# Turning y, output projection, first norm and first feed-forward products in one stage

## The chip, the core and the metric

One Trainium2 chip, one of its cores. The engines are TensorE (PE, matmuls; PEld is its weight load), VectorE (DVE), ScalarE (ACT), GpSimd (POOL) and the sync engine's queue (SP), all working from queues of their own and meeting at semaphores. The metric is the time on the device of one execution of the whole program, in microseconds; lower is better.

## What is computed

Two layers of a hybrid backbone over 9 tiles of 128 tokens (8 of a sample, 1 of a prompt), model width 1024, feed-forward width 4096, all in float32. The part that matters here is the end of a layer:

```
y   = concat(attn 512 | mlstm 256 | gmlp 256) @ w_out
x   = LayerNorm(alpha * x + gate1 * y)
h2  = x * (1 + scale2) + shift2
x   = LayerNorm(alpha * x + gate2 * (relu(h2 @ w_ff1)^2 @ w_ff2))
```

Before it stand the modulation of x, one combined input projection z = h @ w_in, a two-way mLSTM scan, a gated spatial MLP and an attention with axial rotary.

## The kernel before

A product in float32 is made of three matmuls of rounded parts (`product`, L1489): hi*hi, hi*lo and lo*hi. So each operand exists as `hi` (a copy rounded by ScalarE) and `lo` (the difference, by VectorE or GpSimd). Weights come through a ring of four raw slots on SP's queue (L448); `split_hi` (L402, ScalarE) and `split_lo` (L412, VectorE) make the two parts of the eight slots of 128x512 of a group. A slot is refilled once the last tile has used it.

`dense` (L1497) multiplies one tile of 128 tokens by one group: 8 x 3 matmuls of 512 columns into one PSUM bank.

Each layer is cut into eight stages by `phase` (L354): every engine drains, counts up a semaphore, and waits until all four have. The stages that the change touches:

- Stage 1 is the input projection and the mLSTM. GpSimd's queue ends it with the load of zq (L549).
- Stage 2 is the gating part. VectorE takes means and variances of `vn`; GpSimd raises `rs` to the power -0.5 (L478), drains, and makes `nbias` (L554); ScalarE normalises with these, then VectorE and TensorE go on (L1166, L1633).
- Stage 5: TensorE turns y, tile by tile with eight transposes (L1774), ScalarE copies to `hi` (L842), VectorE subtracts to `lo` (L1343). All of y is turned before the barrier.
- Stage 6: GpSimd issues the loads of x (`xr`), of the gates and of `lnb` (L601 to L608). TensorE runs `dense` over the nine tiles for the left half of the output columns, then for the right half. VectorE's `residual` (L1349) makes gate * y and alpha * x + that. After the right half comes the norm, spread over three engines: statistics on VectorE (L949), power and `nbias` on GpSimd (L480), x * rs + nbias on ScalarE (L664), gain on GpSimd (L491), offset on VectorE (L960), store of x1 on GpSimd (L610). Then TensorE turns x (L1788), VectorE modulates it out of PSUM with eight operations a tile (L935), ScalarE rounds (L660), GpSimd subtracts (`lo_of`, L495). There are three bank pairs for turned tiles.
- Stage 7 is the feed-forward in eight chunks of 512 hidden columns. GpSimd begins it with a memset of `acc` (L622), for which VectorE waits before its first hidden tile. `first_product` (L1800) makes twelve blocks of 128 hidden columns by 384 tokens; `second_product` (L1819) makes 18 blocks that VectorE adds to `acc` (`summed`, L1390). After the last chunk comes the second norm with the same helpers as the first, tile by tile, with three banks for TensorE to run ahead; tiles are stored by `store2` (L640).

The order of work on each engine is written out by hand and is the order of the program text. A queue is strictly in order.

Of the kernel before, what the change touches and what calls it, by code (L numbers as in the profile page):

```python
# [17 lines left out]
ALU = mybir.AluOpType  # L18
# [5 lines left out]
P = 128  # L24
# [146 lines left out]
def build(nc, x_in, cond, w_mod, m_slots, b_mod, w_slots, consts, rope, cache_k, cache_v, state0, row_in,  # L171
# [6 lines left out]
    with ExitStack() as ctx:  # L178
# [33 lines left out]
        xr = put("xr", [NT, D])  # L212
        hf2 = put("hf2", [3, D])
        lnb = put("lnb", [2, D])
        gate = put("gate", [2, D])
        lnt = put("lnt", [2, W])
        put = region(a_b + NT * D * 4, a_a)
        f_hi = put("f_hi", [HC // P, TOK], F32R)
        f_lo = put("f_lo", [HC // P, TOK], F32R)
        fr = put("fr", [2, GRP])  # L220
        fsq = put("fsq", [2, GRP])

# [103 lines left out]
        def sem(name):  # L326
# [12 lines left out]
            yT_ps y_hi y_lo o_out xr_half ln_ld xr_done x1_st  # L339
            h_ps r_done fhi_done flo_done f_ps f_acc acc_zero ln_in ln_rs ln_x ln_g y_rdy ln_st""".split()  # L340
# [6 lines left out]
        NB = 8  # L347
# [104 lines left out]
        def _(pool):  # L452
# [27 lines left out]
            def norm_rows(L, w, x, gain, store):  # L480

                for t in range(NT + 2):
                    if t < NT:
                        n, r = NT * (2 * L + w) + t, rs[:, t:t + 1]
                        pool.wait_ge(S["ln_in"], n + 1)
                        pool.tensor_tensor(r, r, half[:, 0:1], ALU.pow)
                        pool.drain()  # L487
                        pool.tensor_tensor(nbias[:, t:t + 1], nmean[:, t:t + 1], r, ALU.mult).then_inc(S["ln_rs"], 1)
                    if 1 <= t <= NT:
                        pool.wait_ge(S["ln_x"], NT * (2 * L + w) + t)  # L490
                        pool.tensor_tensor(x[:, t - 1], x[:, t - 1], gain, ALU.mult).then_inc(S["ln_g"], 1)  # L491
                    if t > 1:
                        store(t - 2)
# [7 lines left out]
            for L in range(NL):  # L501
# [49 lines left out]

                rstd(L, 0, rs[:].unsqueeze(2), 1)
# [46 lines left out]
                phase(pool, L, 5)  # L599

                pool.dma_start(xr[:], (y_out if L else x_in).rearrange("t p d -> p t d")).then_inc(S["ln_ld"], 16)  # L601
                pool.wait_ge(S["mod_st"], stored(L))
                for g in range(2):
                    for n in range(2):
                        pool.dma_start(gate[:, g, n * W:(n + 1) * W],
                                       gate_dram[L, 0, g, n * W:(n + 1) * W].partition_broadcast(P)).then_inc(S["ln_ld"], 16)
                for k in range(2):
                    pool.dma_start(lnb[:, k], ln_gb[L, k].partition_broadcast(P)).then_inc(S["ln_ld"], 16)  # L608

                def store1(t):  # L610
                    pool.wait_ge(S["xr_done"], NT * L + t + 1)
                    own(pool)
                    pool.dma_start(x1_dram[t], xr[:, t]).then_inc(S["x1_st"], 16)

                norm_rows(L, 0, xr, lnb[:, 0], store1)

                for t in range(NT):
                    lo_of(t, hf2[:, t % 3], 2 * NT * L + NT + t)
                pool.wait_ge(S["x1_st"], 16 * NT * (L + 1))
                phase(pool, L, 6)  # L620
# [24 lines left out]
                pool.wait_ge(S["ln_ld"], 16 * (13 * L + 13))  # L645
                norm_rows(L, 1, acc, lnb2[:, 0], store2)
                pool.wait_ge(S["ln_st"], 16 * NT * (L + 1))
                phase(pool, L, 7)
# [3 lines left out]
        def _(act):  # L652
# [11 lines left out]
            def norm_rows(L, w, x):  # L664

                for t in range(NT):
                    act.wait_ge(S["ln_rs"], NT * (2 * L + w) + t + 1)
                    act.activation(x[:, t], x[:, t], ACT.Identity, bias=nbias[:, t:t + 1],
                                   scale=rs[:, t:t + 1]).then_inc(S["ln_x"], 1)
# [37 lines left out]
            for L in range(NL):  # L707
# [131 lines left out]
                for t in range(NT):  # L839
                    act.wait_ge(S["yT_ps"], NT * L + t + 1)  # L840
                    for k in range(2):
                        ins = act.copy(hi[:, 4 * k:4 * k + 4, t * P:(t + 1) * P],  # L842
                                       ps[:, 2 * (t % 3) + k, :].rearrange("p (a b) -> p a b", b=P))
                    ins.then_inc(S["y_hi"], 1)
                phase(act, L, 5)

                split_hi(act, L, 6, (S["o_out"], START + 18 * L + 9))
                norm_rows(L, 0, xr)
                for half_, tiles in ((0, range(3)), (1, range(3, NT))):
                    split_hi(act, L, 7, (S["o_out"], START + 18 * L + 18), range(RAW * half_, RAW * half_ + RAW))  # L850

                    for t in tiles:
                        hi_of(t, hf2[:, t % 3], 2 * NT * L + NT + t)
                phase(act, L, 6)


                def hidden(i, b):
# [5 lines left out]
                    act.activation(f_hi[:, b // 3, (b % 3) * GRP:(b % 3 + 1) * GRP], fr[:, b % 2],  # L863
# [15 lines left out]
                norm_rows(L, 1, acc)  # L879
                if L < NL - 1:  # L880
                    split_hi(act, L, 2 * NFF + 7, (S["f_ps"], START + 18 * NFF * (L + 1)))
                phase(act, L, 7)
# [3 lines left out]
        def _(dve):  # L886
# [62 lines left out]
            def statistics(x, t):  # L949

                dve.drain()
                for j in range(2):
                    dve.bn_stats(st6[:, t, j], x[:, t, j * W:(j + 1) * W])
                dve.drain()
                dve.bn_aggr(mv[:, t], st6[:, t].rearrange("p a b -> p (a b)"))
                dve.drain()
# [8 lines left out]
            for L in range(NL):  # L965
# [394 lines left out]
                for t in range(NT - 1):  # L1360
                    residual(0, t)
# [572 lines left out]
```

## Time and profile before

| | us |
|---|---|
| median of 3 runs | 3694.7 (3691.9 to 3694.89) |
| the profiled execution | 3692.73 |
| its span in the trace | 3690.8 |
| TensorE busy / VectorE / ScalarE / GpSimd | 3205.9 / 1743.1 / 914.2 / 593.4 |

Times in the rows are microseconds from the span's start unless "ns" stands there. Layer 0's stages 5 and 6 lie between 822 and 1000 us, its last chunk with the second norm ends at about 1900; layer 1's lie between 2671 and 2848, and its end is the end of the program. TensorE runs at one of two clocks, 1.2 or 2.4 GHz, and the granted clock averages 0.923 of the full one over the span. A matmul's end is modelled, so the pace of a run is read from the distance of two starts.

### The profile page before, as it was taken

To read this page: it belongs to the slowest core of one execution; us is meant where nothing else is said; L and a number is where in the kernel's file an instruction comes from. 1 tells how busy PE (TensorE), PEld (TensorE's weight loads), DVE (VectorE), ACT (ScalarE), POOL (GpSimd) and SP (SyncE) were. 2 spreads that over 40 slices of the span, in tenths; PEclk is the share of its full clock that TensorE was granted. 3 is DMA by queue.
4 is the path that set the end of the run, shared out by engine and by line. 5 is a ranking of instruction groups with operands and counts; after the bars stand their busy time and mean duration, and the time that the engine had idled before them with its cause. 6 is when DMAs were issued, how large, how long until landed. Compare 5 with 4: busy or idle time off the path is not lost.

```text
span 3690.8 us, 44939 instructions
## 1 busy us (share of the span) xinstructions
PE 3205.9 (87%) x17192; PEld 2577.7 (70%) x17192; DVE 1743.1 (47%) x3144; ACT 914.2 (25%) x1688; POOL 593.4 (16%) x635
## 2 busy tenths in 40 slices
PE   5999649989599999999849996499995999999995
PEld 4778534447488888889838785344474999999994
DVE  4444366654733333333583443666447333333337
ACT  2222124441212211112222221244412222222221
POOL 2010133321600000000150001333216000000004
PEclk7999759999799999999979997599897999999998
DMA  5431300002122222221311113000021111111112
GB/s 191 153 112 52 99 10 1 0 0 103 70 78 81 79 76 76 85 84 35 114 68 34 52 52 99 10 1 0 0 97 74 44 37 35 46 46 46 46 46 114
DMA packets 100547, 225.71 MB, mean 61 GB/s; under 512 B 13168, under 2 KB 13744, under 8 KB 99856
## 3 DMA queue, kind: packets, MB, share of 16 engines
q1 hardware_dynamic: 78240, 151.76, 13.2%
q0 software_dynamic: 22128, 71.50, 5.2%
q8 instruction: 121, 1.98, 0.2%
q14 instruction: 58, 0.48, 0.0%
HBM read 194.33 MB, written 28.87 MB: 60 GB/s over the span
## 4 chain that ended last, share of the span: by engine, by line
PE 67%; issue 11%; DVE 9%; POOL 6%; DMA 3%; POOLq 2%; ACT 2%; DVEq 1%; ACTq 0%; SPq 0%
PE ps L1491 18%; PE ps L1495 17%; PE ps L1494 17%; PE ps L1686 3%; DVE hf L940 2%; PE ps L1665 2%; PE ps L1473 2%; DVE nm L1294 1%; POOL acc L491 1%; PE ps L1676 1%; POOL xr L491 1%; POOLq L487 1%; PE ps L1579 1%; PE ps L1677 1%; PE ps L1633 1%
## 5 line engine op out<-in xcount | busy, mean ns | idle before, releaser
L1491 PE MATMUL ps<-hi,w_hi 128*128 128x384 f32 x1584 | 539.2, 340 | 62.8 <-POOLq L357 44.4
L1495 PE MATMUL ps<-hi,w_lo 128*128 128x384 f32 x1584 | 533.1, 337 | 0.0
L1494 PE MATMUL ps<-lo,w_hi 128*128 128x384 f32 x1584 | 532.7, 336 | 0.0
L1491 PE MATMUL ps<-w_hi,f_hi 128*128 128x512 f32 x1152 | 459.4, 399 | 34.7 <-DVE acc L1395 34.7
L1494 PE MATMUL ps<-w_lo,f_hi 128*128 128x512 f32 x1152 | 453.0, 393 | 0.0
L1495 PE MATMUL ps<-w_hi,f_lo 128*128 128x512 f32 x1152 | 452.4, 393 | 0.0
L410 ACT CAST w_hi<-w_raw 128x512 fp32r<-128x512 f32 x368 | 214.4, 619 | 909.8 <-PE ps L1491 805.7
L1491 PE MATMUL ps<-w_hi,hi 128*128 128x512 f32 (+1 forms) x1008 | 393.0, 390 | 15.1 <-DVE xr L1356 7.4
L1395 DVE TENSOR_TENSOR acc<-acc,ps 128x512 f32<-128x512 f32 x288 | 196.0, 685 | 419.2 <-PE ps L1495 419.0
L1494 PE MATMUL ps<-w_lo,hi 128*128 128x512 f32 (+1 forms) x1008 | 384.3, 381 | 0.0
L1495 PE MATMUL ps<-w_hi,lo 128*128 128x512 f32 (+1 forms) x1008 | 383.9, 381 | 0.0
L415 DVE TENSOR_TENSOR w_lo<-w_raw,w_hi 128x512 fp32r<-128x512 f32 x368 | 261.8, 751 | 200.7 <-ACT w_hi L410 200.3
L1491 PEld LDWEIGHTS ps<-hi,w_hi 128*128 128x128 f32 x1584 | 300.4, 190 | 75.1 <-issue 55.9
L1384 DVE TENSOR_TENSOR fsq<-fr 128x384 f32<-128x384 f32 x192 | 107.0, 557 | 482.7 <-ACT fr L861 482.5
L1494 PEld LDWEIGHTS ps<-lo,w_hi 128*128 128x128 f32 x1584 | 300.2, 189 | 0.5
L1495 PEld LDWEIGHTS ps<-hi,w_lo 128*128 128x128 f32 x1584 | 299.9, 189 | 0.0
L1491 PEld LDWEIGHTS ps<-w_hi,f_hi 128*128 128x128 f32 x1152 | 218.7, 190 | 94.5 <-DVE acc L1395 39.8
L1495 PEld LDWEIGHTS ps<-w_hi,f_lo 128*128 128x128 f32 x1152 | 218.5, 190 | 46.6
L1494 PEld LDWEIGHTS ps<-w_lo,f_hi 128*128 128x128 f32 x1152 | 218.6, 190 | 43.4
L802 ACT ACTIVATE pr<-ps 128x512 f32<-128x512 f32 x292 | 171.2, 598 | 272.9 <-PE ps L1677 270.0
L1491 PEld LDWEIGHTS ps<-w_hi,hi 128*128 128x128 f32 x1008 | 194.1, 193 | 58.6 <-DVE xr L1356 8.3
L861 ACT ACTIVATE fr<-ps 128x384 f32<-128x384 f32 x192 | 94.2, 491 | 517.6 <-PE ps L1495 517.6
(268 smaller groups left out, 4389.8 us busy)
## 6 DMA issues: line engine op xcount, KB each, us to landing
w_raw<-in_w_slots SPq DMA_DIRECT2D x368, 256.0 KB, 3.2
w_raw<-in_m_slots SPq DMA_DIRECT2D x160, 256.0 KB, 2.8
x_dram<-xr POOLq DMA_DIRECT2D x18, 512.0 KB, 3.0
x1t<-x_dram POOLq DMA_DIRECT2D x6, 1536.0 KB, 14.9
out<-acc POOLq DMA_DIRECT2D x18, 512.0 KB, 3.0
modw<-in_w_mod SPq DMA_DIRECT2D x4, 2048.0 KB, 9.8
acc<-in_x_in SPq DMA_DIRECT2D x3, 1536.0 KB, 16.8
zq_dram<-stg POOLq DMA_DIRECT2D x18, 256.0 KB, 2.3
```

What stands on the lines that cost most here:

```text
L410: act.copy(w_hi[:, j, :], w_raw[:, j % RAW, :]).then_inc(S["w_hi_done"], 1)
L415: dve.tensor_tensor(w_lo[:, j, :], w_raw[:, j % RAW, :], w_hi[:, j, :].bitcast(F32), ALU.subtract).then_inc(S["w_lo_done"], 1)
L491: pool.tensor_tensor(x[:, t - 1], x[:, t - 1], gain, ALU.mult).then_inc(S["ln_g"], 1)
L802: act.activation(pr[:, j if nk > 1 else g], ps[:, 3 + (j + g) % 2, :], ACT.Exp).then_inc(S["ex_done"], 1)
L861: act.activation(fr[:, b % 2], ps[:, b % 3, 0:GRP], ACT.Relu).then_inc(S["r_done"], 1)
L940: ins = dve.tensor_scalar(dst[:, u, kt * P:(kt + 1) * P], ps[:, 2 * u + kt // 4, (kt % 4) * P:(kt % 4 + 1) * P], col(L, which, 1, kt, g), ...
L1384: dve.tensor_tensor(fsq[:, b % 2], fr[:, b % 2], fr[:, b % 2], ALU.mult)
L1395: dve.tensor_tensor(a, a, ps[:, 3 + s_ % 3, :], ALU.add).then_inc(S["f_acc"], 1)
L1491: mm = pe.matmul(out, a_hi, b_hi, start=first, stop=False)
L1494: pe.matmul(out, a_hi, b_lo, start=False, stop=False)
L1495: return pe.matmul(out, a_lo, b_hi, start=False, stop=last)
L1686: return pe.matmul(ps[j:j + w, bank, :], weights, moving, start=start, stop=stop)
```

## The change

Stages 5 and 6 and the beginning of stage 7 become one stage without barriers; NB, the barriers per layer, goes from 8 to 6.

- x lives in the rows of z: its left half lies over the columns of mLSTM's q and k, which are unused after stage 1, its right half over the columns that y occupies. The left half and the gates are loaded on GpSimd's queue right after barrier 1 (`xa_ld`), the right half and `lnb` once all of y is turned (`xb_ld`).
- TensorE turns two tiles of y ahead, then one tile before each product; in the second pass it turns a tile of x after each product from the fourth on. Turned tiles have two bank pairs, (3, 4) and (5, 7). The last three tiles of x are turned inside the first feed-forward product, whose order is new (`first_blocks`): the lower halves of the sums of blocks 0 and 1, their upper halves, then block 2.
- The norm: `residual` gives the sum with `accum_out`; VectorE makes the negated mean; ScalarE squares x minus the mean with a sum (`squares`); GpSimd makes 1 / sqrt(variance + eps) (`deviation`); VectorE finishes with two fused operations (`normal`). GpSimd no longer multiplies by the gain. The second norm is changed in the same way.
- The modulation: VectorE takes the left four blocks of a tile (`modulate2`), ScalarE the right four (`modulated`).
- f_hi and f_lo lie in other places, as four tiles each.

```diff
+def first_blocks():
+    lower, upper = range(KT // 2), range(KT // 2, KT)
+    out = [(0, 0, lower), (0, 1, lower), (0, 0, upper), (0, 1, upper), (0, 2, range(KT))]
+    return out + hidden_blocks()[6:]
...
+        NB = 6
+        X_BANKS = ((3, 4), (5, 7))
...
+            def deviation(n, t):
+                r = rs[:, t:t + 1]
+                pool.wait_ge(S["ln_sq"], n + 1)
+                pool.tensor_scalar(r, r, 1.0 / D, EPS, ALU.mult, ALU.add)
+                pool.drain()
+                pool.tensor_tensor(r, r, half[:, 0:1], ALU.pow).then_inc(S["ln_rstd"], 1)
...
                 phase(pool, L, 1)
+                pool.dma_start(x_halves(0), (y_out if L else x_in).rearrange("t p d -> p t d")[:, :, 0:W]).then_inc(S["xa_ld"], 16)
+                pool.wait_ge(S["mod_st"], stored(L))
+                for g in range(2):
+                    for n in range(2):
+                        pool.dma_start(gate[:, g, n * W:(n + 1) * W],
+                                       gate_dram[L, 0, g, n * W:(n + 1) * W].partition_broadcast(P)).then_inc(S["xa_ld"], 16)
                 rstd(L, 0, rs[:].unsqueeze(2), 1)
                 pool.drain()
                 pool.tensor_tensor(nbias[:], nmean[:], rs[:], ALU.mult).then_inc(S["pow_out"], 1)
...
+                pool.wait_ge(S["yT_ps"], NT * (L + 1))
+                own(pool)
+                pool.dma_start(x_halves(1), xin[:, :, W:D]).then_inc(S["xb_ld"], 16)
...
+                for t in range(NT + 4):
+                    if t < NT:
+                        deviation(2 * NT * L + t, t)
+                    if 1 <= t <= NT:
+                        store1(t - 1)
+                    if t >= 4:
+                        lo_of(t - 4, hf2[:, t % 2], 2 * NT * L + NT + t - 4)
...
+            def squares(n, t, x, out):
+                act.wait_ge(S["ln_mu"], n + 1)
+                act.drain()
+                act.activation(out, x, ACT.Square, bias=nmean[:, t:t + 1], accum_out=rs[:, t:t + 1]).then_inc(S["ln_sq"], 1)
...
+                for t in range(NT):
+                    squares(2 * NT * L + t, t, x_row(t), sqr[:].rearrange("p (a b) -> p a b", b=W))
+                    if t == NT - 1:
+                        split_hi(act, L, 7, (S["o_out"], START + 18 * L + 18), range(RAW))
+                    if t >= 4:
+                        modulated(L, t - 4)
+                modulated(L, 5)
+                split_hi(act, L, 7, (S["o_out"], START + 18 * L + 18), range(RAW, SLOTS))
+                for t in range(6, NT):
+                    modulated(L, t)
...
+            def normal(n, t, x, weights, done):
+                dve.wait_ge(S["ln_sq"], n + 1)
+                dve.scalar_tensor_tensor(x, x, nmean[:, t:t + 1], w_row(weights, 0), ALU.add, ALU.mult)
+                dve.drain()
+                dve.wait_ge(S["ln_rstd"], n + 1)
+                dve.scalar_tensor_tensor(x, x, rs[:, t:t + 1], w_row(weights, 1), ALU.mult, ALU.add).then_inc(done, 1)
...
+                for t in range(NT):
+                    residual(1, t)
+                    negated_mean(t, mv[:, t, 0:1], mv[:, t, 1:2])
+                    if t == NT - 1:
+                        split_lo(dve, L, 7, range(RAW))
+                    if t:
+                        normal1(t - 1)
+                    if t >= 4:
+                        modulate2(L, t - 4)
+                modulate2(L, 5)
+                normal1(NT - 1)
+                split_lo(dve, L, 7, range(RAW, SLOTS))
+                for t in range(6, NT):
+                    modulate2(L, t)
...
+                y_turned(0)
+                y_turned(1)
                 for t in range(NT):
+                    if t + 2 < NT:
+                        y_turned(t + 2)
+                    pe.wait_ge(S["y_lo"], START + NT * L + t + 1)
+                    pe.wait_ge(S["xr_half"], START + 18 * L + t - 2)
+                    dense(L, 5, t, t % 3, W, t == 0, t == NT - 1, S["o_out"])
+                for t in range(NT):
+                    pe.wait_ge(S["xr_half"], START + 18 * L + 9 + t - 2)
+                    dense(L, 6, t, t % 3, W, t == 0, t == NT - 1, S["o_out"])
+                    if t >= 3:
+                        x_turned(t - 3)
...
+                        if not i and not m and not ks[0]:
+                            x_turned(6 + g)
+                            pe.wait_ge(S["h_done"], START + 2 * NT * L + NT + 3 * g + 3)
```

## Rows read from the trace of the kernel before

**Rows 1.** The page: the chain that ended last, shares by engine.
```profile
PE 67%; issue 11%; DVE 9%; POOL 6%; DMA 3%; POOLq 2%; ACT 2%; DVEq 1%; ACTq 0%; SPq 0%
```

**Rows 2.** Timeline, TensorE: start, duration, operation, [idle before and releaser].
```profile
822.36 0.63 PE L1774 MATMUL ps<-ident,zq 128*128 128x128 f32 x4 [0.91 <-DVEq L357]
823.26 0.60 PE L1774 MATMUL ps<-ident,zq 128*128 128x128 f32 x4
...
825.91 0.66 PE L1774 MATMUL ps<-ident,zq 128*128 128x128 f32 x4 [0.74 <-DVE lo L1343]
...
835.96 0.79 PE L1491 MATMUL ps<-w_hi,hi 128*128 128x512 f32 x1 [2.98 <-DVEq L357]
...
836.97 0.63 PE L1495 MATMUL ps<-w_hi,lo 128*128 128x512 f32 x1
837.40 0.63 PE L1491 MATMUL ps<-w_hi,hi 128*128 128x512 f32 x1
...
842.89 0.39 PE L1491 MATMUL ps<-w_hi,hi 128*128 128x512 f32 x1
843.11 0.39 PE L1494 MATMUL ps<-w_lo,hi 128*128 128x512 f32 x1
...
859.81 0.80 PE L1491 MATMUL ps<-w_hi,hi 128*128 128x512 f32 x1 [4.52 <-DVE xr L1356]
...
944.09 0.39 PE L1495 MATMUL ps<-w_hi,lo 128*128 128x512 f32 x1
...
999.81 0.66 PE L1491 MATMUL ps<-hi,w_hi 128*128 128x384 f32 x1 [16.63 <-POOLq L357]
```

**Rows 3.** Timeline, VectorE, layer 0's projection and norm.
```profile
858.29 0.69 DVE L1353 TENSOR_TENSOR lnt<-ps,gate 128x512 f32<-128x512 f32 x1 [22.88 <-DMA lnb<-in_ln_gb]
859.07 0.69 DVE L1356 SCALAR_TENSOR_TENSOR xr<-xr,lnt 128x512 f32<-128x512 f32 x1
...
918.09 2.38 DVE L1356 SCALAR_TENSOR_TENSOR xr<-xr,lnt 128x512 f32<-128x512 f32 x1
...
950.94 2.63 DVE L940 TENSOR_SCALAR hf<-ps,modc 128x128 f32<-128x128 f32 x8
```

**Rows 4.** Timeline, GpSimd, layer 0's norm and the feed-forward's start.
```profile
917.51 2.41 POOL L491 TENSOR_TENSOR xr<-xr,lnb 128x1024 f32<-128x1024 f32 x1
...
964.12 6.95 POOL L498 TENSOR_TENSOR lo<-hf,hi 128x1024 fp32r<-128x1024 f32 x3
...
999.72 7.79 POOL L622 MEMSET acc<- 128x9216 f32 x1 [0.52 <-POOLq L357]
```

**Rows 5.** Timeline, VectorE and GpSimd, the end of layer 0.
```profile
1820.10 1.22 DVE L1438 TENSOR_TENSOR acc<-acc,gate 128x1024 f32<-128x1024 f32 x1 [10.28 <-DMA lnb<-in_ln_gb]
...
1866.19 2.95 DVE L1438 TENSOR_TENSOR acc<-acc,gate 128x1024 f32<-128x1024 f32 x1
...
1874.80 2.98 DVE L1438 TENSOR_TENSOR acc<-acc,gate 128x1024 f32<-128x1024 f32 x1
...
1897.33 1.22 DVE L963 TENSOR_TENSOR acc<-acc,lnb 128x1024 f32<-128x1024 f32 x1 [2.23 <-POOL acc L491]
...
1804.19 2.17 POOL L632 DMA_DIRECT2D gate<-gate_dram  x4 [164.14 <-PE ps L1495]
...
1829.34 0.19 POOL L488 TENSOR_TENSOR nbias<-nmean,rs 128x1 f32<-128x1 f32 x1 [4.06 <-issue]
```

**Rows 6.** Timeline, GpSimd, the end of stage 1, layer 0.
```profile
444.64 1.08 POOL L549 DMA_DIRECT2D zq<-zq_dram  x1 [11.84 <-DMA out<-mrow]
```

**Rows 7.** The chain of waits around barrier 1, layer 0: start, duration, what.
```profile
445.72 12.62 POOLq L357
...
464.71 0.21 POOL nbias L554
```

**Rows 8.** Timeline, ScalarE, layer 0.
```profile
953.00 1.24 ACT L668 ACTIVATE xr<-xr,nbias,rs 128x1024 f32<-128x1024 f32 x1 [4.34 <-POOL nbias L488]
...
1015.81 0.49 ACT L861 ACTIVATE fr<-ps 128x384 f32<-128x384 f32 x1 [1.53 <-PE ps L1495]
```

More of the change, by code:

```diff
@@ L612, in store1 @@
                     own(pool)
[L613 to L618, printed above, removed]
+                    pool.dma_start(x1_dram[t].rearrange("p (a b) -> p a b", b=W), x_row(t)).then_inc(S["x1_st"], 16)
+                for t in range(NT + 4):
[5 more added lines that the diff above has]
+                        lo_of(t - 4, hf2[:, t % 2], 2 * NT * L + NT + t - 4)
                 pool.wait_ge(S["x1_st"], 16 * NT * (L + 1))
-                phase(pool, L, 6)
+                pool.wait_ge(S["xT_ps"], 2 * NT * (L + 1))
+                own(pool)
                 pool.memset(acc[:], 0.0).then_inc(S["acc_zero"], 1)
@@ L643, in store2 @@
                     pool.dma_start(y_out[t], acc[:, t]).then_inc(S["ln_st"], 16)
-                pool.wait_ge(S["ln_ld"], 16 * (13 * L + 13))
-                norm_rows(L, 1, acc, lnb2[:, 0], store2)
+                pool.wait_ge(S["ln_ld"], 16 * 6 * (L + 1))
+                for t in range(NT + 1):
+                    if t < NT:
+                        deviation(2 * NT * L + NT + t, t)
+                    if t > 0:
+                        store2(t - 1)
                 pool.wait_ge(S["ln_st"], 16 * NT * (L + 1))
-                phase(pool, L, 7)
+                phase(pool, L, 5)
         @block.scalar
@@ L1358, in _ @@
-                dve.wait_ge(S["ln_ld"], 16 * (13 * L + 7))
-                own(dve)
-                for t in range(NT - 1):
-                    residual(0, t)
-                split_lo(dve, L, 6)
-                residual(0, NT - 1)
-                for t in range(NT + 2):
-                    if t < NT:
-                        residual(1, t)
-                        statistics(xr, t)
-                    if t > 1:
-                        offset(L, 0, xr, t - 2, lnb[:, 1], S["xr_done"])
-                    if t >= NT - 1:
-                        modulate(L, t + 1, 1, hf2, t - (NT - 1), 1)
@@ L1428, in _ @@
                 chunk(NFF - 1)
-                for t in range(NT + 2):
+                for t in range(NT + 1):
                     if t < NT:
@@ L1440, in _ @@
                         dve.wait_ge(x1_ld[t // 3], 16 * (L + 1))
-                        dve.scalar_tensor_tensor(a, x1t[:, t], ALPHA, a, ALU.mult, ALU.add)
-                        statistics(acc, t)
-                    if t > 1:
-                        offset(L, 1, acc, t - 2, lnb2[:, 1], S["y_rdy"])
+                        dve.scalar_tensor_tensor(a, x1t[:, t], ALPHA, a, ALU.mult, ALU.add, accum_out=mv[:, t, 0:1])
+                        negated_mean(t, mv[:, t, 0:1], 0.0)
+                    if t > 0:
+                        normal(2 * NT * L + NT + t - 1, t - 1, y_row(acc, t - 1), lnb2, S["y_rdy"])
                 if L < NL - 1:
                     split_lo(dve, L, 2 * NFF + 7)
-                phase(dve, L, 7)
+                phase(dve, L, 5)
         @block.tensor
```

173 lines of the change are left out of this document (85 added, 88 removed).

## The prediction, made before the changed kernel was run

> **What bounds the kernel now.** I read the page first, its shares by engine in the chain [rows 1]: TensorE is 67% of the chain that ended last, and 11% is "issue". So only time in which TensorE stands still is for sale, and the question is where it stands. The timeline of TensorE answers it for layer 0 [rows 2]: it turns y from 822.36 us, waits 2.98 us for a barrier, multiplies from 835.96, waits 4.52 us at 859.81, ends the second half of the output projection at 944.09, and starts the feed-forward at 999.81. The first three hidden blocks are out, at about 1015.2, just before ScalarE reads the third at 1015.81 [rows 8]. The feed-forward's wait for the barrier alone is 16.63 us. Layer 1 runs through the same code and shows the same order. What stands between is VectorE, ScalarE and GpSimd work [rows 3, 4]. The end of each layer is paced by VectorE [rows 5], and the gating part's short stage by a chain through GpSimd [rows 6, 7].
>
> Two behaviours of the rows decide the sum. First, in [rows 3] a 512-wide two-input VectorE operation takes 0.69 us at 859.07 but 2.38 us at 918.09, where GpSimd's L491 [rows 4] runs from 917.51 for 2.41 us; it ends when that one ends plus its own time. So the two exclude each other. (The Trainium skill, SBUF — State Buffer, section on two separate sides, calls this an exclusive lock between a GpSimd operation and a VectorE one with two SBUF inputs; the trace agrees.) VectorE's modulation, read from PSUM, is not slowed: 0.32 us each [rows 3]. Second, GpSimd's barrier right after its zq load [rows 6] lasts 12.62 us [rows 7], until that load is in; and in [rows 5] the `nbias` at 1829.34 stands behind a drain and that is when the 6.8 MB issued from 1804.19 on (gates, x1t, lnb2: 4 x 256, 3 x 1536, 2 x 512 KB) are through. A drain on GpSimd therefore waits for the DMAs that GpSimd has issued.
>
> **The change, from 822.36 to the end of the first three hidden blocks, per layer.**
> Start. Two tiles of y are turned, 0.9 us each (822.36 to 823.26 is one tile, [rows 2]). The third needs the banks of the first, free at 825.91 as now [rows 2]. The first product starts at 826.9 instead of 835.96: -9.1. Six more turns lie among the products: 6 x 0.9 = +5.4. ScalarE's copies and VectorE's subtractions for them take 1.2 us in a tile period of over 6 and are hidden.
> x. Half of x and the gates are loaded after barrier 1, the other half with lnb once y is turned, some 30 us before the second pass. The wait for the DMA (VectorE at 858.29, [rows 3]) goes: 4.52 us. Behind it TensorE ran at 1.2 GHz (matmuls 0.43 us apart at 836.97, 0.23 at 842.89, [rows 2]) for some 13 matmuls, 13 x 0.2 = 2.6. The low clock of the very first product stays. -7.1.
> Second pass. Six tiles of x are turned in it, five before its end: +4.5. Can VectorE keep up? A tile costs it 0.77 + 0.77 for the residual, 0.2 for the mean, 2.5 for two fused 1024-wide steps (1.23 each [rows 5]; nothing shows one with a sum output, for which I take no extra, and 0.1 each at most), 1.3 for four modulations: 5.6 us against TensorE's 24 x 0.2275 + 0.9 = 6.4 (the matmuls from 842.89 on follow at 0.22 to 0.23). Turn t must wait until tile t-2 has left its two banks. ScalarE's cast closes this 6.7 us after the product's end, about one period, so it is just in time until GpSimd's `lo` of 2.32 us (three in 6.95, [rows 4]) comes in: from then VectorE's two-input steps wait for it, the cast comes after 8.5 to 8.9 us, and two or three periods grow to 7.4: +2.9. The second pass ends at 944.3 - 9.1 + 5.4 - 7.1 + 7.4 = 940.9.
> After it (T). Now: 1015.2 - 944.4 = 70.8 us. After, in VectorE's order, with four splits, 0.62 us apart, waiting for ScalarE's: residual and mean to T+1.8; squares on ScalarE to 3.2 (1.24 for 1024 wide [rows 8]); splits 0 to 3 to 6.8; norm of tile 7 to 9.4; modulation of 4 and 5 to 12.0; cast of 4 to 11.8, `lo` of 4 to 14.2, which holds back the norm of tile 8 to 16.7; GpSimd stores tile 8 before `lo` of 5, which ends at 19.7; splits 4 to 7 to 21.6; modulation of 6 and 7 to 24.2. TensorE meanwhile makes the lower half of the first block, that of the second from 19.7, their upper halves from 21.6 to 27.7 with the low clock, turns tile 8, and this is modulated to 29.9, cast to 31.0, `lo` to 33.4. The third block ends at T+37.5, at the low clock in part T+39. -31.8. ScalarE's four 128-wide steps are not in the trace: from 384 wide 0.49 and 1024 wide 1.24 [rows 8] comes an estimate of 0.2 each, at most 0.49. 0.2 is nearest and VectorE's four take longer; at 0.49 each tile of the tail costs 0.7 more.
> GpSimd's memset of acc (7.79 us [rows 4]) now overlaps TensorE: to T+41.2. VectorE waits for it before its first hidden tile, but three banks let TensorE run on to its sixth block at T+45. No cost here; if the tail came out 5 us shorter, it would begin to show.
> Sum: -9.1 + 5.4 - 7.1 + 7.4 - 31.8 = -35.2 us per layer. Bounds -42 (no exclusion in the tail) and -25 (each of five `lo` operations delays the chain once more).
>
> **The end of a layer.** Now a tile takes VectorE 8.61 us (1866.19 to 1874.80, [rows 5]), with a 2.98 us product [rows 5] held back by GpSimd's gain. That gain, the statistics (about 2.0 in five short operations) and the offset go. After: 1.37 for two sums, 1.30, 1.31, 0.2 for the mean, 2.5 for the norm: 6.7, and 0.3 for GpSimd's single-column steps on `rs` that can come between: 7.0. TensorE needs 5.46 and follows. The start stays (1820.10, [rows 5]: the load's landing). The first norm waits for the drain that ends at 1829.3, so iteration 1 ends at 1831.2; seven more at 7.0 give 1880.2, the last norm 1882.9, in place of the L963 that ends at 1898.5: -15.6. Bounds -12 and -18. ScalarE's squares lie in VectorE's next iteration. Both layers end in the same way.
>
> **Stage 2, gating norm.** The first half of x (2.36 MB) and four gates (1.05 MB) are issued on GpSimd's queue after barrier 1, and behind them stand `rs`, a drain and `nbias`, for which ScalarE, then VectorE, then TensorE wait: `nbias` at 464.71 [rows 7] is in the chain. The issues end by about 461.7 (1.08 for the large one [rows 6], 2.17 for four gates as in [rows 5]) and hide behind VectorE's statistics. The drain does not: 2.36 MB held the barrier for 13.7 us from issue, 6.8 MB held the drain 25.1 us, so 3.4 MB hold it 14 to 16 us from 458.4. `nbias` comes at about 473.2 instead of 464.7: +8.5, bounds 0 and +10. (The Trainium skill, PSUM — Partial Sum Buffer, section on engine and sequencer instructions, says that a drain waits for the engine to go fully idle, and names no DMAs. By it this term would be 0 and the forecast 17 us lower; [rows 5, 7] speak against that reading.)
> Two barriers go; their waits are counted above.
>
> **The sum.** -35.2 - 15.6 + 8.5 = -42.3 per layer, -85 for both. Profiled execution: 3692.7 us (span 3690.8) gives 3607.7; the median of the runs, 3694.7, stands 2 us higher, so 3610.
>
> **The rivals.**
> A: the drain does not wait for DMAs (a large DMA only holds a barrier). Then stage 2 costs nothing: 3610 - 17 = 3593. For it: only one long drain outside a barrier is among the rows. Against: its end falls on the end of the transfers. Chance 0.12.
> B: the exclusion and the two bank pairs bite harder. Each x turn waits for cast and `lo` in series, the second pass goes at 9 us a tile for five tiles, and the tail gets five delays: -25 and -12 in place of -35.2 and -15.6, 13.8 a layer, 3638. For it: both orders are strict and every engine waits for another. Against: the PSUM reads and ScalarE do not contend. Chance 0.2.
> C, slower: the clock. The merged stage's stops are short but frequent. If the clock stayed at 1.2 GHz throughout, 432 matmuls would cost 0.2 us more each, 86 us a layer. It decides from half of them: 43 us a layer cancel the gain. All of them would give 3610 + 2 x 86 = 3782; the likely form of this case, six tenths of them, 3713. Against: the stop of 2.98 us in [rows 2] lowered it for under 7 us (835.96 to 842.89), and the stops expected here are shorter. Chance 0.03.
> D: the tail does not shorten, since the feed-forward's start hangs on tile 8 anyway: it takes 55 us in place of 39. Then -19.2 in the merged stage: 3642. Against: only the third block needs tile 8, and 8 us of products come before. Chance 0.1.
> The forecast has 0.55.
>
> **How the numbers follow.** Range: A at 3593 less the better bounds gives 3575 at the outside, B and D with stage 2 at its upper bound 3645. With 2 in 10 left out: 3580 to 3640. All cases but C are faster by far more than 0.2%, about what a measurement of this kernel can tell from none. Faster 0.96, same 0.01, slower 0.03.
>
> **What would show it.** Between the second pass's last product and the third hidden block some 39 us; no TensorE wait for a DMA in the merged stage; second-pass periods of 6.4 growing to 7.4; `nbias` of stage 2 some 8 us later, behind GpSimd's drain; VectorE's last tiles 7.0 us apart, and no GpSimd operation 1024 wide among them. The prediction is wrong if TensorE waits over 1.5 us at each turn of x, if the low clock covers over a third of the merged stage, or if VectorE's fused steps with a sum take clearly more than 0.69 and 1.23 us.

## The result: 3595 us, inside the range

| | before | after |
|---|---|---|
| median (runs) | 3693.3 (4) | 3595.1 (4; 3590.7 to 3599.8) |
| span of the profiled execution | 3690.8 | 3588.9 |
| TensorE / VectorE / ScalarE / GpSimd busy | 3205.9 / 1743.1 / 914.2 / 593.4 | 3168.6 / 1680.1 / 939.4 / 529.0 |

The ratio is 0.9739, with a 95% interval of 0.9719 to 0.9759. The forecast was 3610, the range 3580 to 3640. All times in this text are of fast executions; one execution below, the profiled one of the kernel with two waits less, was a slow one (10900.3 us beside 3553.0 to 3556.4 for its other five), so its trace is not read. On the page the chain that ended last, by engine, reads now (before: [rows 1]):

```profile
PE 73%; DVE 8%; issue 7%; POOL 3%; DMA 3%; ACT 2%; POOLq 2%; DVEq 1%; ACTq 0%; SPq 0%
```

TensorE has more of the chain and "issue" less, as a kernel with fewer stops should show. TensorE is also busy for 37 us less with the same products and turns: from the first turn of y to the third hidden block of layer 0 its granted clock averages 0.94, where it was 0.82.

**The merged stage, layer 0.** TensorE's timeline (start, duration, operation, [idle before and releaser]) answers [rows 2]:

```profile
833.26 0.63 PE L1847 MATMUL ps<-ident,zq 128*128 128x128 f32 x4 [0.91 <-DVEq L400]
...
837.66 0.47 PE L1563 MATMUL ps<-w_hi,hi 128*128 128x512 f32 x1
...
838.44 0.40 PE L1563 MATMUL ps<-w_hi,hi 128*128 128x512 f32 x1
...
839.13 0.40 PE L1563 MATMUL ps<-w_hi,hi 128*128 128x512 f32 x1
...
943.33 1.06 PE L1855 MATMUL ps<-ident,xr 128*128 128x128 f32 x8 [1.20 <-ACT hi L708]
...
950.82 1.06 PE L1855 MATMUL ps<-ident,xr 128*128 128x128 f32 x8 [0.96 <-ACT hi L708]
961.11 1.94 PE L1855 MATMUL ps<-ident,xr 128*128 128x128 f32 x8 [9.23 <-ACT hi L708]
...
969.38 0.44 PE L1563 MATMUL ps<-hi,w_hi 128*128 128x384 f32 x1 [2.22 <-POOL lo L534]
...
982.38 0.69 PE L1563 MATMUL ps<-hi,w_hi 128*128 128x384 f32 x1 [5.13 <-POOL lo L534]
...
988.68 0.44 PE L1563 MATMUL ps<-hi,w_hi 128*128 128x384 f32 x1
```

Read it as three stretches. From the first turn of y (833.26) to the first product (837.66) there are 4.4 us. To the last product's end at 949.9 (the T of the prediction) it is 116.6 us from the start. From there to the end of the third hidden block at 988.4, just before the fourth begins at 988.68, it is 38.5 us. TensorE waits for no DMA on the way. In all 155.1 us, where the kernel before took 193.4 (822.36 to 1015.8, where ScalarE begins to read the third block, [rows 2, 8]): -38.3. The prediction put that end at 1015.2, 0.6 us too early.

What sets the pace in the second pass is in VectorE's and GpSimd's timelines; the first of each group answers to [rows 3] and [rows 4]:

```profile
920.51 0.69 DVE L1416 TENSOR_TENSOR lnt<-ps,gate 128x512 f32<-128x512 f32 x1 [2.03 <-PE ps L1567]
...
926.84 0.69 DVE L1416 TENSOR_TENSOR lnt<-ps,gate 128x512 f32<-128x512 f32 x1 [0.71 <-PE ps L1567]
927.61 2.61 DVE L1419 SCALAR_TENSOR_TENSOR xr<-xr,lnt 128x512 f32<-128x512 f32 x1
930.15 0.08 DVE L1419 DVE_READ_ACCUMULATOR xr<-xr,lnt 128x1 f32 x1
...
934.29 0.68 DVE L1416 TENSOR_TENSOR lnt<-ps,gate 128x512 f32<-128x512 f32 x1
...
942.16 0.69 DVE L1416 TENSOR_TENSOR lnt<-ps,gate 128x512 f32<-128x512 f32 x1
...
943.86 3.10 DVE L1015 SCALAR_TENSOR_TENSOR xr<-xr,nmean,lnb 128x1024 f32<-128x1024 f32 x1
```

```profile
927.30 2.38 POOL L534 TENSOR_TENSOR lo<-hf,hi 128x1024 fp32r<-128x1024 f32 x1 [0.93 <-ACT hi L708]
...
943.28 2.60 POOL L534 TENSOR_TENSOR lo<-hf,hi 128x1024 fp32r<-128x1024 f32 x1 [1.15 <-ACT hi L708]
...
979.98 2.35 POOL L534 TENSOR_TENSOR lo<-hf,hi 128x1024 fp32r<-128x1024 f32 x1 [2.17 <-ACT hi L708]
982.26 7.79 POOL L664 MEMSET acc<- 128x9216 f32 x1
```

The residuals of successive tiles begin 6.33, 7.45 and 7.87 us apart. The 2.61 us operation at 927.61 stands in for one of 0.69, and it ends at 930.22, 0.54 us after GpSimd's `lo` of 927.30 is through (929.68). The same stands at 943.86: 3.10 for 1.28, under the `lo` of 943.28.

**The end of layer 0**, VectorE [rows 5]:

```profile
1793.03 1.23 DVE L1510 TENSOR_TENSOR acc<-acc,gate 128x1024 f32<-128x1024 f32 x1 [10.69 <-DMA lnb<-in_ln_gb]
...
1802.93 1.29 DVE L1018 SCALAR_TENSOR_TENSOR acc<-acc,rs,lnb 128x1024 f32<-128x1024 f32 x1 [1.89 <-POOL rs L529]
...
1818.73 1.22 DVE L1510 TENSOR_TENSOR acc<-acc,gate 128x1024 f32<-128x1024 f32 x1
...
1825.34 1.23 DVE L1510 TENSOR_TENSOR acc<-acc,gate 128x1024 f32<-128x1024 f32 x1
...
1852.16 1.28 DVE L1018 SCALAR_TENSOR_TENSOR acc<-acc,rs,lnb 128x1024 f32<-128x1024 f32 x1 [0.46 <-POOL rs L529]
```

A tile takes 6.61 us in place of 8.61, none of its two-input operations is stretched (the longest takes 1.29 us for one), and the stretch from the first tile to the last norm is 60.4 us instead of 78.4: -18.0.

**Stage 2, layer 0**, the chain of waits in order of time (start, duration, what), which answers [rows 7]:

```profile
446.93 1.07 POOL zq L585
448.00 13.72 POOLq L400
...
462.41 1.02 POOL xr L588
463.43 2.18 POOL gate L592 x4
...
466.05 1.89 POOLq L595
467.94 6.71 issue
...
474.68 0.20 POOL nbias L596
```

The power ends at 467.94, and for 6.71 us nothing of the chain runs: GpSimd stands in its drain while the x and gate loads are under way. Layer 1 shows the same, 6.81 us. Below, this time between the power and `nbias` is called the hold.

The balance is -38.3 - 18.0 + 6.6 = -49.7 us for layer 0. For layer 1 the same three places give about -37.2, -19.4 and +6.7. That is -99.6 us of the span's -101.9. The good fit is in part chance: outside the three places layer 0 came out 4.6 us longer and layer 1 6.9 us shorter. Most of that lies ahead of stage 2 or in stages 3 and 4, and single profiles scatter there: kernels that share all code up to the load of zq issue it in layer 0 anywhere from 444.75 to 451.80. What moved these stretches is not settled.

### The profile page after: what moved, and what is told of

It is laid out like the page before. It is cut to its first block, busy times and chain, and to the rows that moved or that the text cites. A ratio compares the mean times of both kernels' runs of the same rounds, so it can differ in the third digit from the quotient of the medians.

```text
span 3588.9 us, 44827 instructions
## 1 busy us (share of the span) xinstructions
PE 3168.6 (88%) x17192; PEld 2549.8 (71%) x17192; DVE 1680.1 (47%) x3018; ACT 939.4 (26%) x1796; POOL 529.0 (15%) x601
## 4 chain that ended last, share of the span: by engine, by line
PE 73%; DVE 8%; issue 7%; POOL 3%; DMA 3%; ACT 2%; POOLq 2%; DVEq 1%; ACTq 0%; SPq 0%
PE ps L1563 20%; PE ps L1567 19%; PE ps L1566 19%; PE ps L1758 3%; PE ps L1737 2%; PE ps L1545 2%; DVE nm L1359 1%; PE ps L1748 1%; DVE hf L998 1%; PE ps L1651 1%; PE ps L1749 1%; PE ps L1705 1%; POOL dg L620 1%; PE ps L1674 1%; PE ps L1669 1%
## 5 line engine op out<-in xcount | busy, mean ns | idle before, releaser
L458 DVE TENSOR_TENSOR w_lo<-w_raw,w_hi 128x512 fp32r<-128x512 f32 x368 | 246.7, 711 | 201.9 <-ACT w_hi L453 201.5
```

What stands on the lines that cost most here:

```text
L458: dve.tensor_tensor(w_lo[:, j, :], w_raw[:, j % RAW, :], w_hi[:, j, :].bitcast(F32), ALU.subtract).then_inc(S["w_lo_done"], 1)
```

## Experiments

What each should tell apart. My theory has four parts: the drain pays for loads that are under way (term +8.5); the exclusion between GpSimd's `lo` (the subtraction that makes the low half of a tile) and VectorE is what stretches the second pass; the fused norm pays at the end of the layer; the new order of the first blocks is what shortens the tail. The ratios are all against the kernel before, run beside each kernel on the same chip; the kernel before itself had medians of 3684.9 to 3692.5 us there, so medians from different chips differ by some us for that alone.

**The kernel after once more**, as the reference for the small differences.

> The changed kernel as it is, on the same chip as the next three, for differences of less than 1%. Every theory: about 3595 us as before, and in stage 2 of both layers a hold of 6.7 us at GpSimd's drain between the power of rs and nbias.

Measured: 3593.9 us, ratio 0.9739 (0.9720 to 0.9759), holds of 7.33 us in layer 0 and 6.89 in layer 1. The numbers of the result stand.

**The loads behind `nbias`.**

```diff
-pool.dma_start(x_halves(0), ...).then_inc(S["xa_ld"], 16)
-...
 rstd(L, 0, rs[:].unsqueeze(2), 1)
 pool.drain()
 pool.tensor_tensor(nbias[:], nmean[:], rs[:], ALU.mult)
+pool.dma_start(x_halves(0), ...).then_inc(S["xa_ld"], 16)
+...
```

> The five loads of x's left half and the gates are issued after nbias instead of before rs. Theory (GpSimd's drain waits for the DMAs that GpSimd has issued): the hold of 6.7 us per layer goes, the loads now end behind the 22 us of stage 2, so 13 us less than the changed kernel. Rival (the drain is long for another reason, or the time comes back at barrier 2 or with the loads of stage 3): within 3 us of the changed kernel.

Measured: 3580.9, ratio 0.9698 (0.9677 to 0.9719), so 13.1 us less than the kernel after. The drain now takes 0.16 us. This shows that the loads ahead of the drain cost the time, but not how: they could slow the engine's work, or the drain could wait for them.

**The loads stay, the drain goes.** The power counts a semaphore and `nbias` waits for this.

```diff
-rstd(L, 0, rs[:].unsqueeze(2), 1)
-pool.drain()
+rstd(L, 0, rs[:].unsqueeze(2), 1).then_inc(S["own_p"], 1)
+pool.wait_ge(S["own_p"], L + 1)
```

> The loads stay before rs; between the power and nbias GpSimd waits for a semaphore that the power itself counts up, instead of a drain. Theory (the drain waits for the DMAs, not for the engine's own operation): nbias follows the power within 0.3 us although the loads are in flight; 13 us less than the changed kernel, as with late loads. Rival (traffic of 3.4 MB slows GpSimd or the visibility of its results, whichever way it waits): nbias stays some 6 us behind the power, no gain.

Measured: 3577.8, ratio 0.9697 (0.9678 to 0.9716), 16.2 us less than the kernel after. GpSimd's timeline, with the loads in flight:

```profile
462.16 1.02 POOL L588 DMA_DIRECT2D xr<-in_x_in  x1 [13.91 <-POOLq L400]
463.18 2.17 POOL L592 DMA_DIRECT2D gate<-gate_dram  x4
465.85 1.84 POOL L521 TENSOR_TENSOR rs<-rs,half 128x9 f32<-128x9 f32 x1 [0.50 <-DVE rs L1225]
467.78 0.20 POOL L596 TENSOR_TENSOR nbias<-nmean,rs 128x9 f32<-128x9 f32 x1
```

`nbias` follows the power at once although 3.4 MB are moving. The two holds of the kernel after sum to 14.2 us, near enough to the 16.2 (15.5 by the ratios). So the traffic slows nothing in this chain; it is the drain that waits. Rival A of the prediction (the drain doesn't wait for DMAs) is refuted, and the Trainium skill's words on the drain (PSUM — Partial Sum Buffer, section on engine and sequencer instructions), read as naming the engine's work alone, don't cover this case.

**Only the gates behind `nbias`**, a dose: 2.36 MB are in front of the drain in place of 3.4.

> Only the four gate loads (1.05 of 3.41 MB) move behind nbias, x's left half stays before rs. Theory (the hold lasts until the issued bytes are in, at some 0.4 MB a us): 1.05 MB is 2.6 us of transfer, so the hold falls from 6.7 to 3.5 to 4.5 us and the kernel gains 4 to 6 us over both layers. Rival (a fixed cost of any drain behind a DMA): the hold stays 6.7 us. Rival (it is the partition-broadcast of the gates that is slow): the hold falls to under 1 us.

Measured: 3584.7, ratio 0.9723 (0.9702 to 0.9744); holds of 4.46 and 4.01 us. GpSimd in layer 0:

```profile
459.08 1.02 POOL L588 DMA_DIRECT2D xr<-in_x_in  x1 [13.26 <-POOLq L400]
462.77 1.84 POOL L521 TENSOR_TENSOR rs<-rs,half 128x9 f32<-128x9 f32 x1 [2.67 <-DVE rs L1225]
469.07 0.21 POOL L591 TENSOR_TENSOR nbias<-nmean,rs 128x9 f32<-128x9 f32 x1 [4.46 <-issue]
```

The trace has the one load in front of the drain land 9.8 us after its issue at 459.08, at 468.9, and `nbias` starts 0.2 us later; in layer 1 it is 9.4 us from 2250.53, and `nbias` starts at 2260.06, 0.1 us later. So the hold ends with the landing. 1.05 MB fewer take 2.9 us off each hold, about what the transfer of these needs at the 0.4 MB a us of this stretch. The time fell by 9.3 us and the holds by 5.75; the rest is within what two kernels' medians leave open (about 4 us).

**The second norm alone**, put into the kernel before.

```diff
 for t in range(NT + 1):
     ...
-    dve.scalar_tensor_tensor(a, x1t[:, t], ALPHA, a, ALU.mult, ALU.add)
-    statistics(acc, t)
+    dve.scalar_tensor_tensor(..., accum_out=mv[:, t, 0:1])
+    negated_mean(t, mv[:, t, 0:1], 0.0)
+    if t > 0: normal(NT * L + t - 1, t - 1, ...)
```

> The kernel before with one part of the change: the second norm in fused form (sum in the residual, squares on ScalarE, two fused steps on VectorE, no gain on GpSimd). Theory: the end of each layer is VectorE's and its tiles go from 8.6 to 6.6 us; 18 us per layer as in the changed kernel's trace, so some 36 us less than the kernel before (0.990). Rival (the gain at a layer's end needs the merged stage, through x1's earlier stores or loads): under 20 us less.

Measured: 3644.7 beside 3684.9, ratio 0.9883 (0.9865 to 0.9901): -40 us by the medians, -43 by the ratio and -36 at the interval's weak end. The end of layer 0 on VectorE:

```profile
1823.46 1.23 DVE L1478 TENSOR_TENSOR acc<-acc,gate 128x1024 f32<-128x1024 f32 x1 [10.03 <-DMA lnb<-in_ln_gb]
...
1882.55 1.28 DVE L998 SCALAR_TENSOR_TENSOR acc<-acc,rs,lnb 128x1024 f32<-128x1024 f32 x1 [0.46 <-POOL rs L509]
```

From the first tile's start to the last norm's end at 1883.83 it is the 60.4 us of the kernel after again. This norm alone is over a third of the whole gain, and it is independent of the merged stage.

**`lo` of the turned x tiles on VectorE**, not on GpSimd, so that no 1024-wide GpSimd operation stands in the stage.

```diff
-lo_of(t - 4, hf2[:, t % 2], 2 * NT * L + NT + t - 4)      # GpSimd
+dve.tensor_tensor(lo[:, :, t * P:(t + 1) * P], hf2[:, t % 2], hi[...], ALU.subtract)
```

> The changed kernel with the subtraction hi to lo of the nine x tiles in the merged stage on VectorE (1.2 us each) instead of GpSimd (2.3 us and held or holding). Theory (GpSimd and VectorE exclude each other, so GpSimd's operation costs VectorE its whole length anyway): second pass about as now, the piece from its last product to the third hidden block shrinks from 38.6 to about 34 us, 6 to 12 us less than the changed kernel in all. VectorE's two-input steps of 2.6 to 3.2 us are gone. Rival (VectorE is simply full, and GpSimd's work was mostly beside it): 5 us or more slower than the changed kernel.

Measured: 3584.4, ratio 0.9722 (0.9704 to 0.9739) beside 0.9739. By the medians some 10 us are gone and by the ratios 6, but the intervals overlap, so the trace must decide. In it no two-input operation of VectorE in this stage takes over 1.29 us, the subtraction takes 1.22 us where GpSimd's took 2.4 to 3.5, and the last wait of TensorE is shorter (3.96 us in place of 5.13):

```profile
962.32 1.94 PE L1867 MATMUL ps<-ident,xr 128*128 128x128 f32 x8 [10.38 <-ACT hi L706]
...
980.17 0.45 PE L1575 MATMUL ps<-hi,w_hi 128*128 128x384 f32 x1 [3.96 <-DVE lo L1438]
```

The third block ends 36 us after the last product in place of 38.5, and the second pass ends 1.4 us earlier; its periods are 6.36, 7.06, 7.49 and 7.08. From the first turn of y to the fourth block it is 151.7 us in place of 155.4, in layer 1 149.9 in place of 154.5. So the exclusion is real, but getting rid of it in this way brings only some 4 us a layer, since the moved work costs VectorE 1.22 us a tile. The periods still grow to 7.1 and more, so the exclusion is not all that stretches the second pass: VectorE's own work fills these tiles. No run takes the exclusion away without giving VectorE more to do, so what it costs by itself is not measured.

**The old order of the hidden blocks**, in the merged stage.

```diff
-hidden_blocks() if i else first_blocks()
+hidden_blocks()
```

> The changed kernel with the first feed-forward product in the old order of blocks (three lower halves, then three upper halves). Theory (only block 2 needs tile 8, and whatever is queued behind its wait comes late): the upper halves of blocks 0 and 1, 2 x 2.1 us, move behind the wait for the last lo, 4.2 us per layer, 8 us slower than the changed kernel. Rival (the start of the feed-forward hangs on tile 8 alone): no change beyond 2 us.

Measured: 3597.3, ratio 0.9760 (0.9743 to 0.9776), +3.4 us by the medians and +7.8 by the ratios. TensorE's wait for tile 8 is 6.40 us, and the upper halves of blocks 0 and 1 stand behind it:

```profile
980.57 0.69 PE L1563 MATMUL ps<-hi,w_hi 128*128 128x384 f32 x1 [6.40 <-POOL lo L534]
```

ScalarE reads the third block at 992.41, 42.4 us after the last product. The order is worth 2 to 4 us a layer of a tail that was 71 us in the kernel before; most of the shortening comes without it.

**All eight modulation steps on VectorE.**

```diff
-for kt in range(KT // 2): dve.tensor_scalar(hf2[...], ps[...], ...)
-for kt in range(KT // 2, KT): act.activation(hf2[...], ..., ACT.Identity, bias, scale)
+for kt in range(KT): dve.tensor_scalar(hf2[...], ps[...], ...)
```

> The changed kernel with all eight modulation steps of a tile on VectorE, none on ScalarE. Theory (VectorE's queue is the longest chain in the second half of the pass and in the piece after it): 1.3 us more in some three periods of the pass and in five tiles after it, 8 to 12 us per layer, 16 to 24 us slower than the changed kernel. Rival (the waits are set by ScalarE's cast and its four slower steps of 1.49 us, so sharing gives little): under 6 us slower.

Measured: 3612.1, ratio 0.9796 (0.9779 to 0.9813), +18.2 by the medians and +21 by the ratios. TensorE's waits at the turns grow, and two more turns run at the low clock (1.90 and 1.94 us for 1.06):

```profile
927.49 1.06 PE L1849 MATMUL ps<-ident,xr 128*128 128x128 f32 x8 [1.83 <-ACT hi L708]
...
936.10 1.90 PE L1849 MATMUL ps<-ident,xr 128*128 128x128 f32 x8 [2.08 <-ACT hi L708]
...
954.21 1.94 PE L1849 MATMUL ps<-ident,xr 128*128 128x128 f32 x8 [2.98 <-ACT hi L708]
965.37 1.94 PE L1849 MATMUL ps<-ident,xr 128*128 128x128 f32 x8 [9.22 <-ACT hi L708]
```

Here VectorE is the bound of the second pass, with 8.6 to 9.5 us a tile. The share given to ScalarE is a large part of what makes the merged stage fit: undoing it costs the merged stage some 9 us a layer, twice what taking `lo` to VectorE gained.

**A better version.** If drains on GpSimd wait for its transfers, the barrier behind stage 1 loses most: there the drain stands behind the 2.36 MB load of zq, for 12.62 us in the kernel before [rows 6, 7] and 13.72 in the one after. Four kernels follow it up, each on top of the last, and the first on top of the kernel with its own semaphore. First the load of zq goes behind `nbias`.

```diff
-pool.dma_start(zq[:], ...).then_inc(S["zq_ld"], 16)
 phase(pool, L, 1)
 rstd(...); pool.wait_ge(S["own_p"], L + 1); pool.tensor_tensor(nbias[:], ...)
+pool.dma_start(zq[:], ...).then_inc(S["zq_ld"], 16)
```

> The kernel after with GpSimd's power counted by a semaphore of its own (as in e2_own_semaphore) and, in addition, the load of zq (2304 KB) issued behind the negated bias and no longer just ahead of the barrier that ends stage 1. In the traces so far GpSimd issues this load at 446.93 and its drain in the barrier ends 13.7 us later (12.6 in layer 1), when the load lands; VectorE idles 18.4 us in front of stage 2. Theory (a drain on GpSimd waits for the DMAs that GpSimd issued): with no load in flight the drain takes about 0.6 us, VectorE starts stage 2 about 14 us earlier in each layer, the load hides behind stage 2 (22 us long, while 5.8 MB take about 15 us at the 390 GB/s of this stretch), so -26 to -28 us against e2_own_semaphore: about 3550. Rival (the barrier itself takes 12 us after a long stage, or another engine comes last): the drain stays above 10 us and the time stays near 3578. Second rival (5.8 MB do not land in time): the load hides badly, the barrier behind stage 2 is held up to 10 us, 3560 to 3572.

Measured: 3561.0, ratio 0.9646 (0.9633 to 0.9659), 16.7 us less than the kernel with its own semaphore by the medians and 19 by the ratios, against the 26 to 28 of the theory. The chain of waits tells where the rest is:

```profile
436.78 12.48 DMA out<-mrow
...
449.48 5.63 POOLq L400
...
455.24 0.43 DVE st L1219
```

GpSimd's last store has landed (449.26) and the zq load is not yet issued, still its drain takes 5.63 us, and 3.66 in layer 1. From the issue of that store to stage 2's first operation it is 18.5 and 17.2 us now, against 27.6 and 28.0 with the load in front: 9.1 and 10.8 us gained. The direction is confirmed; the size was wrong, because I took the whole of the drain for the load's. The second rival (the load hides badly) is refuted: the next barrier comes 28.2 us after stage 2's start, as before.

Then two waits at the end of the layer: the drain between the two steps of each `deviation`, and VectorE's wait for the second norm's weights, which now stands at the first operation that reads them.

```diff
-pool.tensor_scalar(r, r, 1.0 / D, EPS, ALU.mult, ALU.add)
-pool.drain()
+pool.tensor_scalar(...).then_inc(S["own_d"], 1)
+pool.wait_ge(S["own_d"], n + 1)
...
-dve.wait_ge(S["ln_ld"], 16 * 6 * (L + 1))
+dve.wait_ge(S["ln_ld"], 16 * 4 * (L + 1))
...
+if t == 1: dve.wait_ge(S["lnb_ld"], 16 * 2 * (L + 1))
```

> e9_zq_late with two more waits of the end of the layer taken away: GpSimd's drain between the two steps of each deviation is a semaphore of its own, and VectorE's first tile waits for the four loads that it reads, no longer for the two loads of the second norm's weights as well. The profile of after has VectorE idle 10.7 us in front of the first tile of layer 0, ended by the weights' load, and 1.9 us in front of the first norm's second step. Theory: 4 to 10 us less than e9_zq_late in all, about 3543. Rival (the loads of the tiles themselves, in the same queue just ahead of the weights, come last): under 2 us.

Measured: 3554.9, ratio 0.9625 (0.9612 to 0.9638), 6.1 less, as expected. The next kernel holds the same edits, and its trace shows them.

Then `lo` on VectorE again.

> e6_all_waits with the low halves of the turned x tiles taken on VectorE in place of GpSimd (as in e4_lo_on_vector). If the gains are independent: 5 to 10 us less than e6_all_waits, about 3536. Rival (an earlier end of the layer is eaten by a later wait): under 2 us less.

Measured: 3547.2, ratio 0.9606 (0.9593 to 0.9619), 7.7 less: the gains add up. VectorE's timeline at the end of layer 0 shows what the step before did: in place of the one wait of 10.69 us for the weights it waits 3.50 for the gates and 2.43 for x1t, which come in one queue ahead of the weights, and the 1.89 us in front of the first norm's second step are gone:

```profile
1767.22 1.23 DVE L1521 TENSOR_TENSOR acc<-acc,gate 128x1024 f32<-128x1024 f32 x1 [3.50 <-DMA gate<-gate_dram]
...
1770.88 1.23 DVE L1524 SCALAR_TENSOR_TENSOR acc<-x1t,acc 128x1024 f32<-128x1024 f32 x1 [2.43 <-DMA x1t<-x_dram]
```

Last, the remainder of the drain behind stage 1. GpSimd has waited for the landing of its last stores, the last transfers that it issued, so it can count the barrier without a drain.

```diff
-eng.drain().then_inc(S["phase_end"], 1)     # GpSimd, barrier behind stage 1
+pool.sem_inc(S["phase_end"], 1)
```

> e10_all_and_lo with GpSimd's drain in the barrier behind stage 1 taken away: what GpSimd issued before it are transfers whose landing it has already waited for, so it counts the barrier directly. In e9_zq_late this drain still took 5.6 us in layer 0 and 3.7 in layer 1, although the last transfer of GpSimd had landed at its start (449.26) and nothing of the software queue moved afterwards; only SyncE's loads did. VectorE's own last step before the barrier ends at 450.5 and its drain about 0.4 to 0.9 us later. Theory (the remainder is a cost of GpSimd's drain itself after its transfers): stage 2 starts 3.5 to 4.5 us earlier in layer 0 and 2 to 3.5 in layer 1, about 6 to 8 us in all, 3540. Rival (the barrier waits for the loads of SyncE or for another engine just as long): no change, within 1.5 us of 3547.

Measured: 3540.1, ratio 0.9603 (0.9577 to 0.9628), 7.1 less by the medians; the ratios don't tell it from the kernel before it (1 us), since the kernel before, run beside it, was 6 us faster too. The trace does: VectorE starts stage 2 right behind its own drain.

```profile
450.58 3.04 DVE L1218 BATCH_NORM_STATS2 st<-vn 128x6 f32<-128x256 f32 x9 [0.24 <-DVEq L400]
```

From the issue of the last store to this row it is 14.5 us, and 13.1 in layer 1: 4.0 less in both layers than in the kernel with the late zq load, which has the drain. In layer 0 the barrier behind stage 2 now ends with GpSimd's own drain, 28.9 us after the stage's start where it was 28.2: the 5.8 MB of loads in front of that drain only just hide. What the drain behind stage 1 waited for in its 5.6 and 3.7 us isn't settled. GpSimd's last stores had landed by the semaphore, and only SyncE's weight loads moved; in layer 0 their last packet lies over 2 us before the drain's end, in layer 1 some still move when it ends. This last kernel is the fastest here, 3540 us, 4.0% less than the kernel before and 1.4 points more than the change alone.

## Why the prediction was right, step by step

| step | predicted | measured, layer 0 |
|---|---|---|
| first turn of y to first product | 4.5 | 4.4 |
| first turn of y to the last product (T) | 118.5 | 116.6 |
| T to the third hidden block | 39 | 38.5 |
| merged stage | -35.2 | -38.3 |
| end of the layer | -15.6 | -18.0 |
| stage 2 | +8.5 | +6.6 |
| per layer | -42.3 | -49.7 |

All three terms erred to the same side, 7.4 us a layer, and that is the 15 us between 3610 and 3595. Inside the merged stage the fit is better than its parts: a low clock that went and was not counted on (2.6 us), against longer periods.

*Until T.* The start and the vanished wait for x came as worked out. What the sum had not: the first product's low clock goes too. I wrote that it stays, because [rows 2] had it; but there a stop of 2.98 us at the barrier stood ahead of it (granted clock 0.58 from 835.9 to 842.9), and in the merged stage only one of 1.61 us does (1.00 from 837.6 to 844.6). No run takes this stop away alone, so that it was the cause is argued. In the rows above the starts of every third matmul are 0.69 us apart from 838.44 on, which is 0.23 each, the high clock. The 13 slow intervals of the kernel before had cost 2.6 us. The periods were 6.33, 7.45, 7.87 and 7.74 where I had 6.4 growing to 7.4; the stalls at x turns sum to 4.4 us (0.55, 1.71, 1.20, 0.96), of which 3.5 lie before T, against 2.9. The exclusion, named as the cause of the growth, is there, but the kernel with `lo` on VectorE shows that VectorE's load is the other part of it. Two things came on top. The fused step with a sum costs 0.08 on VectorE and 0.18 on ScalarE for reading the sum out. And ScalarE's four modulation steps take 1.49 us:

```profile
923.83 1.49 ACT L722 ACTIVATE hf<-ps,modc 128x128 f32<-128x128 f32 x4
```

That is 0.37 each, between my 0.2 and the bound of 0.49. The step was taken from the wrong end of its bounds.

*The tail.* The three landmarks of the forecast came out: block 1's lower half begins at T+19.5 (worked out 19.7), the last `lo` is done at T+32.5 (33.4), the third block at T+38.5 (39). The second trace of the same kernel has the last two 1.6 and 2.7 us later in layer 0, so an agreement to half a microsecond is partly luck. The memset on GpSimd ended at T+40.2; VectorE waited for it, TensorE did not, as said.

*The end of the layer.* 6.61 us a tile, not 7.0: I added 0.3 for GpSimd's single-column steps, and the rows show that these don't delay VectorE. They are the ones delayed: L527 takes 1.04 to 1.29 us here, and its shortest in the whole trace is 0.19. Seven tiles at 0.39 less are 2.7 us, which covers the 2.4 that were missing.

*Stage 2.* The mechanism was right and the size 1.9 us too large (a hold of 6.74 where the kernel before had 0.16; 6.8 to 7.4 in the other traces). I had scaled the time from issue to the drain's end from two points, 13.7 us at 2.36 MB and 25.1 at 6.8 MB. The first of them held more than the load, for even with none in flight this barrier's drain takes 5.6 us. From issue to the drain's end the same 2.36 MB take 14.8 us in the barrier (446.93 to 461.72) but 10.0 in stage 2 (459.08 to 469.05, the kernel with the gates late), and the 3.4 MB take 12.25 where I had 14 to 16.

*The rivals.* A is refuted by three kernels together: the loads late, the own semaphore, and the gates late. B had the mechanism that exists, at a quarter of its price: TensorE waits 3.5 us at the turns of the second pass, not 13 (five tiles at 9 in place of 6.4). C: the low clock was seen only at single turns and for some 3 us behind each of the waits of 9.23 and 5.13 us; the granted clock averages 0.78 behind T. D: the tail shortened, and by the old-order run even without the new order (42.4 us, where D had 55).

## What to carry to other kernels

Before a load is moved to an earlier place in a queue, look for the next drain on that queue: here the whole landing time stood in the way of a 0.2 us operation, and a semaphore of its own bought it back; the same look at the other drains of the kernel found more than the change had lost. A stop at a stage boundary had the low clock behind it here, so taking it away paid twice (4.5 us of waiting and 2.6 of slow matmuls at the wait for x, 3.0 and 2.6 at the barrier). Between two engines that exclude each other, moving an operation to the other engine pays little (4 us a layer here) where a fusion that makes one vanish pays more (18, though that fusion also takes work off VectorE, and no run separates the two).

## What the runs showed of the hardware beyond the forecast

- A drain on GpSimd waits for the transfers that GpSimd issued: 6.7 to 7.4 us behind 3.4 MB, 4.0 to 4.5 behind 2.36 MB, ended within 0.2 us of that load's landing, 0.16 with none, and 11.2 to 13.8 in the barrier behind the zq load. A semaphore of the instruction itself costs 0.1 us with the same transfers under way.
- Such a drain in a barrier took another 5.6 and 3.7 us after the last of GpSimd's stores had landed, so landing is not all that a drain waits for; what it waits for there stays open.
- Under the exclusion with VectorE it is also GpSimd's single-column steps that grow: 1.50 for 0.56 us at 947.24 of layer 0, beside VectorE's two-input step. (The Trainium skill, SBUF — State Buffer, section on two separate sides, says that whichever of the two starts first keeps the shared ports for its whole instruction; the VectorE step of 947.03 had started first, so the trace agrees.)
- Reading out a sum (`accum_out`) costs 0.08 us on VectorE and 0.18 to 0.19 on ScalarE, and doesn't slow the operation itself.
